# Seven half-size products in place of eight in the FFNs' projections down, with the combinations of the hidden rows made ahead and kept split in DRAM

## The reference, cut to what matters

```
def swiglu_ffn(u, w_in, w_out):
    gate, up = jnp.split(u @ w_in, 2, axis=-1)
    return (jax.nn.silu(gate) * up) @ w_out

h = h + 0.5 * swiglu_ffn(rmsnorm(h, ffn1_norm), ffn1_w_in, ffn1_w_out)
h = h + stick_breaking_attention(rmsnorm(h, mix_norm), sb_w_qkv, sb_w_o)
h = h + 0.5 * swiglu_ffn(rmsnorm(h, ffn2_norm), ffn2_w_in, ffn2_w_out)
return rmsnorm(h[frames], final_norm)
```

## Time and profile before

| what | value |
|---|---|
| time, median of 3 executions | 2048.18 us (2047.39 to 2053.92) |
| profiled execution | 2051.71 us, of which the span from first to last instruction is 2049.9 us |
| TensorE busy | 1969.3 us, 96% of the span, 12868 matmuls recorded |
| VectorE, ScalarE, GpSimd busy | 1105.9, 638.5, 952.4 us |
| mean granted TensorE clock | 0.993 |
| DMA | 167.74 MB, 25.6% of 16 DMA engines |

### The profile page before, as it was taken

The page is one execution under the profiler, slowest core; times in us unless marked ns, Lnnn a source line. Parts: engine busy times, 40 slices in busy tenths (PEclk is TensorE's granted clock), DMA queues, the critical chain, the costliest instruction groups (busy, mean ns, idle before and its releaser), DMA issues.

```text
span 2049.9 us, 35208 instructions
## 1 busy us (share of the span) xinstructions
PE 1969.3 (96%) x12868; PEld 1789.7 (87%) x12868; DVE 1105.9 (54%) x1599; ACT 638.5 (31%) x1115; POOL 952.4 (46%) x698
## 2 busy tenths in 40 slices
PE   7899999999999998999989999989999999999998
PEld 6899999999999988999989986777777777788886
DVE  5755555554555548433389870284444444444445
ACT  5422222222112125222267751242222222221212
POOL 4354545454434425444476761354545454453440
PEclk9999999999999999999999999999999999999999
DMA  4222222223322211333322121012222222242222
GB/s 125 62 68 87 67 87 67 87 70 127 125 83 82 96 28 47 101 103 115 101 95 73 62 70 45 21 36 87 67 87 67 87 75 83 92 140 101 82 92 82
DMA packets 165366, 167.74 MB, mean 82 GB/s; under 512 B 7984, under 2 KB 130864, under 8 KB 165312
## 3 DMA queue, kind: packets, MB, share of 16 engines
q1 hardware_dynamic: 165312, 166.99, 25.6%
HBM read 126.74 MB, written 40.22 MB: 81 GB/s over the span
## 4 chain that ended last, share of the span: by engine, by line
PE 48%; issue 27%; POOL 15%; DVE 4%; ACT 2%; DMA 2%; POOLq 0%; SPq 0%; DVEq 0%; ACTq 0%
PE psum L1360 15%; PE psum L1361 15%; PE psum L1362 15%; POOL arena L551 13%; PE psum L1387 2%; PE psum L1580 1%; DVE arena L1221 1%; DVE arena L1081 1%; POOL arena L567 1%; DMA scratch<-w_out_dram 1%; DMA scratch<-w_o_dram 0%; DVE plain L1071 0%; POOL arena L646 0%; DVE arena L1207 0%; ACT arena L713 0%
## 5 line engine op out<-in xcount | busy, mean ns | idle before, releaser
L1360 PE MATMUL psum<-arena 128*128 128x260 f32 (+3 forms) x4028 | 1288.0, 320 | 48.6 <-POOL arena L551 17.7
L1362 PE MATMUL psum<-arena 128*128 128x260 f32 (+3 forms) x4028 | 1266.8, 314 | 0.0
L1361 PE MATMUL psum<-arena 128*128 128x260 f32 (+3 forms) x4028 | 1265.4, 314 | 0.0
L1360 PEld LDWEIGHTS psum<-arena 128*128 128x128 f32 x4028 | 761.7, 189 | 116.5 <-issue 26.8
L1362 PEld LDWEIGHTS psum<-arena 128*128 128x128 f32 x4028 | 761.3, 189 | 47.2
L1361 PEld LDWEIGHTS psum<-arena 128*128 128x128 f32 x4028 | 761.2, 189 | 46.5 <-issue 3.6
L551 POOL TENSOR_TENSOR arena<-scratch,arena 128x512 fp32r<-128x512 f32 x365 | 511.6, 1425 | 564.8 <-ACT arena L756 564.8
L1119 DVE SCALAR_TENSOR_TENSOR h<-psum,h 128x260 f32<-128x260 f32 (+1 forms) x496 | 250.1, 505 | 212.1 <-PE psum L1362 212.1
L756 ACT ACTIVATE arena<-scratch 128x512 fp32r<-128x512 f32 x371 | 211.9, 622 | 482.4 <-DMA scratch<-w_in_dram 255.1
L1134 DVE TENSOR_TENSOR scratch<-scratch 128x512 f32<-128x512 f32 x200 | 236.8, 1184 | 213.2 <-POOL arena L551 191.1
L1131 DVE TENSOR_TENSOR scratch<-scratch,psum 128x520 f32<-128x520 f32 (+1 forms) x265 | 182.6, 689 | 311.9 <-PE psum L1362 297.0
(11 more groups left out here) (79 smaller groups left out, 1018.8 us busy)
## 6 DMA issues: line engine op xcount, KB each, us to landing
scratch<-w_in_dram SPq DMA_DIRECT2D x88, 512.0 KB, 4.9
scratch<-w_out_dram SPq DMA_DIRECT2D x22, 1024.0 KB, 4.8
qkv<-scratch SPq DMA_DIRECT2D x48, 260.0 KB, 2.1
scratch<-w_qkv_dram SPq DMA_DIRECT2D x24, 512.0 KB, 4.6
scratch<-qkv SPq DMA_DIRECT2D x24, 512.0 KB, 3.8
hidden<-scratch SPq DMA_DIRECT2D x44, 260.0 KB, 2.1
scratch<-hidden SPq DMA_DIRECT2D x11, 1040.0 KB, 5.0
hidden<-scratch SPq DMA_DIRECT2D x44, 256.0 KB, 2.1
```

What stands on the lines that cost most here:

```text
L1360: nc.tensor.matmul(dst, wh, xh, start=start, stop=False, skip_group_check=True)
L1361: nc.tensor.matmul(dst, wh, xl, start=False, stop=False, skip_group_check=True)
L1362: return nc.tensor.matmul(dst, wl, xh, start=False, stop=stop, skip_group_check=True)
```

## The change

Hidden tiles 1 to 20 form ten pairs, and two pairs form a group (`GROUPS` is 5). The projection down of a group to the two d_model tiles d and d + 4 is now a `down_unit`: seven products of halves (halves of d_model, and of rows), of 2 hidden tiles each: 12 matmuls of 260 columns a product in FFN1, 6 of 512 in FFN2. There are 4 down units a group, `DOWN_UNITS` 20 for each FFN. Tiles 0 and 21 go through a plain turn as before (192 and 96 matmuls). The hidden rows' combinations (T1 to T4 as differences, both tiles' halves as B11 to B22) are made in the gate and up units, a pair of units for one pair of tiles, by VectorE (`first_tile`, `second_tile`), split by ScalarE and by VectorE and GpSimd (`pair_rows_lo`), and stored in `pairs_dram` as 14 parts of 128 x 520 or 512; SyncE loads them split, straight to the inputs' regions (`load_pairs`, seven loads of 1040 or 1024 KB a group). The weights of w_out are loaded, combined and split per down unit (two loads of 256 KB; 4 combinations of 128x256, 7 copies, 7 subtractions). VectorE takes each product out of PSUM (`take`), products 0 and 1 into a sum that is added to `h` in the last group. The last FFN2 turn now has 16 groups of matmuls in place of 32 with the output's transposes between them.

```diff
--- before.py
+++ after.py
+HIDDEN_PAIRS = 10
+GROUPS = HIDDEN_PAIRS // 2
+DOWN_UNITS = GROUPS * HK
+DOWN_ORDER = (0, 1, 3, 2, 4, 5, 6)
+DOWN_FREE = (1, 1, 2, 2, 3, 6, 7)
-OUT_AT = {17: ((0, 0), (0, 1)), 20: ((1, 0), (1, 1)), 23: ((2, 0), (2, 1)), 25: ((3, 0), (3, 1)),
-          29: ((4, 0), (5, 0)), 30: ((6, 0),), 31: ((7, 0), (4, 1), (5, 1), (6, 1), (7, 1))}
+OUT_AT = {9: ((0, 0), (0, 1)), 11: ((1, 0), (1, 1)), 13: ((2, 0), (2, 1)),
+          15: ((3, 0), (3, 1)) + tuple((t, half) for half in range(2) for t in range(4, 8))}
...
             def ffn(n):
-                s = ffns[n]
+                s, first_down = ffns[n], PRODUCTS * UNITS[n]
                 load_first(n)
                 store_plain(n)
-                with sp_eng.Fori(0, UNITS[n] - 1) as u:
-                    load_weights(n, u + 1)
-                    store_hidden(n, u)
+                load_weights(n, 1)
+                with sp_eng.Fori(0, HIDDEN_PAIRS - 1) as i:
+                    load_weights(n, 2 * i + 2)
+                    store_first(n, i)
+                    load_weights(n, 2 * i + 3)
+                    store_second(n, i)
+                    store_high(n, i)
+                    store_rest(n, i)
+                load_weights(n, UNITS[n] - 1)
+                store_first(n, HIDDEN_PAIRS - 1)
+                def room_free(products):
+                    sp_eng.wait_ge(s["used"], PRODUCTS * (UNITS[n] - 1) + products)
                 sp_eng.wait_ge(s["w_lo"], PRODUCTS * (UNITS[n] - 1) + 5)
                 sp_eng.wait_ge(s["mixed"], 4 * UNITS[n])
-                load_down(n, 0)
+                load_down_weights(n, 0, 0, 0, 0)
+                pairs_stored(n, HIDDEN_PAIRS - 1)
+                sp_eng.wait_ge(stored_first, 64 * HIDDEN_PAIRS * (n // 2 + 1))
+                store_second(n, HIDDEN_PAIRS - 1)
+                room_free(1)
+                load_pairs(n, 0, 0, (0, 1))
+                store_high(n, HIDDEN_PAIRS - 1)
+                room_free(2)
+                load_pairs(n, 0, 0, (2, 3))
+                store_rest(n, HIDDEN_PAIRS - 1)
+                sp_eng.wait_ge(s["w_loaded"], 32 * UNITS[n] + 32)
+                load_down_weights(n, 1, 0, 1, 1)
+                room_free(3)
+                load_pairs(n, 0, 0, (4, 5))
+                room_free(4)
+                load_pairs(n, 0, 0, (6,))
+                store_last(n)
+                pairs_stored(n, HIDDEN_PAIRS)
+                def next_weights(u, group, d):
+                    sp_eng.wait_ge(s["w_lo"], first_down + PRODUCTS * (u + 1))
+                    sp_eng.wait_ge(s["w_loaded"], 32 * UNITS[n] + 32 * (u + 2))
+                    load_down_weights(n, u + 2, group + (d + 2) // HK, (d + 2) % HK, d % 2)
+                with sp_eng.Fori(0, GROUPS // 2) as i:
+                    for room in range(2):
+                        group = 2 * i + room
+                        sp_eng.wait_ge(s["used"], first_down + PRODUCTS * HK * group)
+                        for d, places in enumerate(((0, 1), (2, 3), (4, 5), (6,))):
+                            next_weights(HK * group + d, group, d)
+                            load_pairs(n, group + 1, 1 - room, places)
+                u = DOWN_UNITS - HK
+                next_weights(u, GROUPS - 1, 0)
                 sp_eng.wait_ge(s["stored"], 64)
-                load_hidden(n, 0)
-                store_hidden(n, UNITS[n] - 1)
-                sp_eng.wait_ge(s["stored"], 32 * FF_TILES)
+                load_hidden(n)
+                next_weights(u + 1, GROUPS - 1, 1)
+                sp_eng.wait_ge(s["h_lo"], 1)
+                load_down(n)
+                sp_eng.wait_ge(s["w_lo"], first_down + PRODUCTS * DOWN_UNITS)
...
+            def pair_rows_lo(n, pair):
+                half, hi = HALF[n], HI_ALL * (n // 2) + 7 * pair
+                for at, (raw, high) in enumerate(((r1, g1), (r0, g0), (x3, x1))):
+                    if at == 1:
+                        pool.wait_ge(made, MADE_ALL * (n // 2) + 4 * pair + 4)
+                    pool.wait_ge(pair_hi, hi + 5 + at)
+                    nc.gpsimd.tensor_tensor(raw[:, 0:half].bitcast(F32R), raw[:, 0:half], high[:, 0:half], ALU.subtract)\
+                        .then_inc(pair_lo_pool, 1)
...
+                def ffn_unit(u, second, pair, last=False):
+                    act.wait_ge(s["used"], PRODUCTS * u)
+                    weight_hi(n, 3)
+                    if not second:
+                        second_rows_high(u, pair)
+                    copy_x(u)
+                    if second:
+                        first_difference_high(pair)
+                    else:
+                        differences_high(pair)
+                    if not last:
+                        act.wait_ge(s["w_loaded"], 32 * u + 64)
+                        weight_hi(n, 0)
+                    if not second:
+                        last_difference_high(pair)
+                    act.wait_ge(s["mixed"], 4 * u + 4)
+                    product_over(u, 3)
+                    weight_hi(n, 6)
+                    first_out(u, None if second else pair)
...
+                def second_tile(u, pair):
+                    dve.wait_ge(s["hid1"], u)
+                    difference(r1, c22, r1)
+                    dve.wait_ge(pair_lo, 4 * pairs_to(pair) + 2)
+                    difference(r0, c22, r0)
+                    dve.wait_ge(made, 4 * pairs_to(pair) + 3)
+                    dve.wait_ge(pair_hi, 7 * pairs_to(pair) + 4)
+                    low(c22, c22, x2)
+                    dve.wait_ge(stored_first, 64 * pairs_to(pair + 1))
+                    difference(x3, u0, r0)
+                    dve.wait_ge(made, 4 * pairs_to(pair) + 4)
+                    low(u0, u0, x1)
...
+                def ffn_unit(u, second=False, pair=None, last=False):
...
+                    if last:
+                        dve.wait_ge(s["hid0"], u + 1)
+                        clear(sums_b[1], taken)
+                        mix_down_last(n, 0, 0)
+                    if pair is not None and not second:
+                        dve.wait_ge(stored_high, 32 * pairs_to(pair + 1))
+                        dve.wait_ge(pair_lo_pool, 3 * pairs_to(pair) + 1)
+                    add(g1, xy, "c", "c12")
+                    if last:
+                        dve.wait_ge(s["c12"], u + 1)
+                        clear(sums_b[0], taken)
+                        dve.wait_ge(s["stored"], 48)
+                        clear(sums_b[3], taken)
+                    dve.wait_ge(s["silu1"], u + 1)
+                        if pair is not None:
+                            dve.wait_ge(stored_last, 64 * pairs_to(pair + 1))
+                    nc.vector.tensor_tensor(out[:, 0:half], g1[:, 0:half], c22[:, 0:half], ALU.mult)\
+                        .then_inc(s["hid1"], 1)
+                    if last:
+                        dve.wait_ge(s["hid1"], u + 1)
+                        clear(sums_b[2], sums_added)
...
+            def mix_down(n, u, j):
+                s, at = ffns[n], 4 * (u + UNITS[n])
+                a11, _, a21, _, _, a22, _ = sources_b(j)
+                dve.wait_ge(s["w_loaded"], 32 * (u + UNITS[n] + 1))
+                dve.wait_ge(s["w_lo"], PRODUCTS * (u + UNITS[n] - 1) + (6 if isinstance(u, int) and u == 0 else 3))
+                nc.vector.tensor_tensor(s3_b, a11, a21, ALU.subtract).then_inc(s["mixed"], 1)
+                dve.wait_ge(s["mixed"], at + 1)
+                nc.vector.tensor_tensor(a21, a21, a22, ALU.add).then_inc(s["mixed"], 1)
+                dve.wait_ge(s["mixed"], at + 2)
+                nc.vector.tensor_tensor(s2_b, a21, a11, ALU.subtract).then_inc(s["mixed"], 1)
+            def mix_down_last(n, u, j):
+                s, a12 = ffns[n], sources_b(j)[4]
+                dve.wait_ge(s["mixed"], 4 * (u + UNITS[n]) + 3)
+                dve.wait_ge(s["w_lo"], PRODUCTS * (u + UNITS[n]))
+                nc.vector.tensor_tensor(s4_b, a12, s2_b, ALU.subtract).then_inc(s["mixed"], 1)
+            def down_unit(n, u, d, final=False, more=True):
+                s, half = ffns[n], HALF[n]
+                front = TAKEN_ALL * (n // 2) + SUMS_CLEARED + PRODUCTS * u
+                quarter = {(far, late): h[:, d + HK * far, late * half:(late + 1) * half]
+                           for far in range(2) for late in range(2)}
+                common = sums_b[d][:, 0:half]
+                def take(place, dst, bank, behind=None):
+                    dve.wait_ge(s["used"], PRODUCTS * (u + UNITS[n]) + place + 1)
+                    if behind is not None:
+                        dve.wait_ge(taken, front + behind)
+                    nc.vector.scalar_tensor_tensor(out=flat(n, dst), in0=target(n, bank), scalar=0.5, in1=flat(n, dst),
+                                                   op0=ALU.mult, op1=ALU.add).then_inc(taken, 1)
+                if d == 2:
+                    dve.wait_ge(sums_added, SUMS_ALL * (n // 2) + 1)
+                take(0, common, "a", behind=0)
```

(24 more changed lines are left out.)

548 lines of the change are left out of this document (360 added, 188 removed).

## The result

The changed kernel takes 2027.04 us (median of 4 runs, 2025.34 to 2030.45) beside 2051.05 us for the kernel before on the same chip (2047.39 to 2055.14): ratio 0.9877, 95% interval 0.986 to 0.9895. It is faster, by 1.2% where 2.6% was predicted. The profiled execution took 2026.75 us with a span of 2024.8, 25.1 less than before; the sum had said 51.4 less.

What follows compares the result with a forecast made beforehand. TensorE was taken to bound FFN1's units and both projections down, a cycle on the weights FFN2's units. Terms summed to -51.4 us, span 2049.9 to 1998.5, forecast 1997 us; its own range 1985 to 2010, overall 1974 to 2030.

Steps and rivals of the forecast that it cites:

- matmuls, both FFNs: Projections down: 240 fewer matmuls in FFN1 save 29.0 us, 120 fewer in FFN2 save 27.8 us.
- FFN2's units: Gate and up units of FFN2 fall from 20.05 to 19.04 us each, -17.2 us over 17 units.
- units to down, both: Turn from units to down units: first down unit stalls behind queued loads and stores, +7.8 us FFN1, +9.2 FFN2.
- last group and plain turn: Ends of the projections down: +0.6 us for FFN1's plain turn, +0.5 each FFN for splitting hidden tiles.
- the end: Behind the last product: 12.0 us become 18 for norm and scaling, two transpose stops saved: +4 us.
- the walk through a pair: Step-by-step timing of two FFN2 gate and up units, giving units of 19.04 us.
- So product 6 need not wait: FFN2's second unit of a pair: GpSimd's low part 6 ends at T+14.6, needed at T+16.3.
- gain nothing: Rival: FFN2's units gain nothing, or lose up to 8 us: 2013 to 2021 us; chance 0.20.
- the long stop: Fourth product of each FFN's first down unit: one stall of some 10 us, ended by a store's landing.
- +0.5 each FFN: Down unit: splitting hidden tiles, 4 x 1.29 us on GpSimd, costs 0.5 us in each FFN.
- +0.6: FFN1's plain turn starts behind three sums of 0.69 us, costing 0.6 us.
- (3, 4): Slower rivals: every down-unit combination collides at 1.77 us, 2076 us, chance 0.07; pair loads at half rate, 2086 us, 0.04.

Runs made afterwards that it cites:

- e2_omit: Changed kernel with GpSimd's three subtractions per pair (low parts of T3, T2, T4) done on only 8 columns: 2015.93 us.
- e3_r1room: Changed kernel with the last quarter's sums gathered in r1, not u0, so the third clearing waits for the last pair's stores: 2017.06 us.
- e4_actq: Changed kernel with the store of the last hidden tile's first half issued by ScalarE when ready, not by SyncE behind the seven loads: 2017.1 us.
- e12_no_hidden_lo: Changed kernel with GpSimd's subtraction for the last hidden tiles done on only 8 columns a tile: 2023.13 us.
- e9_place: Changed kernel with hidden tiles' low parts in four pieces behind the next unit's fourth weight low part, QKV plain weights' behind FFN1's last sums: 2026.17 us.
- e8_tail: Changed kernel with FFN2's closing transposes after groups 8, 10, 12, 14 in place of 9, 11, 13, 15: 2028.65 us.
- e5_pieces: Changed kernel with GpSimd's long subtractions for the last hidden tiles and the plain turn's down weights each cut in four: 2028.59 us.
- e14_place2: Changed kernel with e3_r1room's edit, e9_place's QKV wait, and the hidden tiles' four pieces directly behind the next unit's third combination: 2009.89 us.
- e10_both: Changed kernel with the edits of e3_r1room and e9_place together: 2016.03 us.

## Why the prediction was right in direction and wrong in size

By its own terms, in us (measured from matmul starts in the two profiles: stops longer than a pitch, plus what matmuls at the lower clock take above the usual pitch):

```
                              predicted   measured
matmuls, both FFNs              -56.8      -58.7    29.5 and 29.2
FFN2's units                    -17.2       -7.8
units to down, both             +17.0      +25.9    13.4 and 12.5
last group and plain turn        +1.6      +14.3     9.9 and 4.4
the end                          +4.0       +6.3
QKV, attention (no change)          0       -4.5
sum                             -51.4      -24.5    span: -25.1
```

**Matmuls: right.** FFN1 takes 1872 x 0.1195 us in place of 2112 x 0.1199, FFN2 936 x 0.2299 in place of 1056 x 0.2314. The rate of 0.1208 that the sum took from the earlier trace rows was slightly high, since its window, 500 to 750 us, takes in the start of the norm, where from 743.6 us on matmuls start 0.219 us apart.

**FFN2's units: the step that failed is the walk through a pair, "So product 6 need not wait".** In the profile, with T 1426.5 us as the start of a second unit and the walk's time in brackets: the first unit's four low parts ended at T+3.0 (1.4), its last combination at T+3.6 (1.8), the second load was issued at T+4.5 (2.6), low part 0 began at T+10.2 (8.1), the three subtractions took 4.25 us (3.9) and ended at T+15.7 (13.3), low part 6 took 1.71 (1.3) and ended at T+17.4 (14.6), where 16.3 was needed. Of the 2.8 us, 0.8 are collisions of the last four subtractions, whose price (1.72 us for a low part) stood in the rows. The other 2.1 come round the cycle. The walk let every first unit begin afresh ("the next unit is again paced by product 3"), with its weights landed at T+8.9; in the profile they landed 10.6 us into it (unit of 1446.8 us). It also had the store of B21 land at T+10.0, where VectorE waited for it until T+12.4. e2_omit shows that the wait goes with the three subtractions (low part 6 then ends at T+15.0); that the 2.1 us are there without them too shows that they are not theirs. What makes up the 2.1 us no run takes apart. The units gained 7.8 of 17.2 us, about half way to the case "gain nothing" that I had given 0.20.

**Units to down: right mechanism for the long stop, term too small.** Its place, order and releaser were as forecast: the fourth product, line 1541, the store behind the loads (e3_r1room, e4_actq). The stops in all are near the forecast too: more by 8.4 us than before in FFN1 (7.8 predicted) and by 11.1 in FFN2 (9.2). What had no term is the clock: matmuls at its lower level behind the stops take 5.3 us more in FFN1 and 3.3 in FFN2, where 1.9 of it was there before too. That the stops add up so well is in part luck. The short stop had no term either, and with the slow matmuls behind it it moved the long one from T+24.5 to 30.3 (T: 473.8 us), while the store landed 5.1 us later than forecast, at T+39.8 and not 34.7. The store was issued at 501.2 and not at 493: its half was made at 496.5, since the silu waited for the stores of T3 and T2, and SyncE was held 6.2 us by two loads of weights and 4.1 by three of pairs, instructions that it otherwise issues in 0.4 us. The Trainium skill, DMA: Bandwidth & Descriptors, Queues, rings and completion order, has each engine consume one issuer's descriptors in ring order; the trace agrees: the store issued last of SyncE's before the stop ended landed last, at 513.6, and from ScalarE's ring it passed them. The order of landing is not exact: in e3_r1room the store, issued 0.5 us behind the seventh load, landed 0.3 us before it (512.5 and 512.9).

**Last group: the failed steps are "+0.5 each FFN" for splitting the hidden tiles and "+0.6" for the plain turn.** Both counted VectorE's and GpSimd's work and not the two side by side. I had bounded collisions by 1.77 us from rows in which GpSimd's instructions last 1.3 (median); beside one of 5.2 us a hold is 3.5. The Trainium skill, SBUF — State Buffer, Who interferes with whom, has the second to start block until the first ends: the trace agrees, the combination of 688.29 ended at 691.77, the subtraction at 691.49. The rule, applied to the longest subtraction and not to that of 0.65 us, would have shown the stop. Each of the three stops was followed by matmuls at the lower clock, some 4 of the 14.3 us, for which the sum had no term here either. e12_no_hidden_lo confirms it by taking the subtraction away, for the part in line 1588; for the plain turn's stop e9_place shows that the neighbour was line 711.

**The end:** 19.5 us follow the start of the last product, 12.4 before; the stops for transposes saved 0.7 and not 2. What sets it beyond "four tiles behind the last product" was not settled; e8_tail shows only that tile 3's place does not.

Of the rivals, the stores did not pass the loads (1), and the slower ones (3, 4) did not come: VectorE's four combinations of a down unit last 0.43 to 0.78 us on average where 1.6 would have taken the gain back, loads of pairs land in 8.4 to 8.6 us (median), well inside a group.

## What to carry to other kernels

Walk a tight cycle at the prices that its operations have beside their neighbours, and walk it round until it closes: a unit that ends late hands its lateness to the next one's loads. Follow every semaphore that an operation waits for, the landing of a store in a filled queue too. Where two engines read SBUF side by side, cutting or moving the longer operation only moves the hold, unless the other engine reads PSUM or idles there (e5_pieces, e9_place, e14_place2). And a stop of TensorE can cost more than its length: look at the granted clock behind it.

## What was unexpected of the hardware

The length of a stop of TensorE does not tell whether the granted clock falls behind it. Behind stops of 3.1 to 11.8 us at the ends of its stages in the changed kernel, 5 to 26 matmuls ran at 1.2 GHz. So they did behind stops of 2.2 us at 702.1 us in e9_place and at 694.1 us in e10_both, where the clock was at 0.5 for some 3 us. Behind 2.64 us at 682.8 us in e14_place2, 3.38 us at 491.1 us before and 3.42 us at 1940.2 us in e2_omit it stayed at 1.00. Nothing here says what decides.

SyncE's issue of a DMA, 0.4 us as a rule, took up to 5.3 us when ten transfers of 0.25 to 1 MB were under way (491.8 us in the changed kernel).
